# One gate block ahead of the first prompt tile, and twelve quarters beside it, in the later token groups of a hybrid decoder layer

## The reference, cut to what matters

```python
xn = _rms_norm(h, norm_mix)
qa, ka, va, qkv_b, z, a, b, gate_logits = split(xn @ w_in)
oa = sliding_window_attention(rope(qa), rope(ka), va, sinks)
cb = silu(short_conv(qkv_b))                    # 4 taps; q, k, v of the delta branch
ob = gated_delta(l2norm(q), l2norm(k), v, g, beta)   # chunks of 64 tokens, state S carried on
ob = gated_rms_norm(ob, z)
ga, gb = split(sigmoid(gate_logits), 2)         # 2 x 1024 columns
h = h + (ga * (oa @ w_oa) + gb * (ob @ w_ob)) @ w_out
h = h + (silu(rms(h) @ w_gate) * (rms(h) @ w_up)) @ w_down
```

## Time and profile before

| | |
|---|---|
| median of three runs | 3521.89 us |
| profiled execution, its own time | 3523.42 us |
| its span | 3521.6 us |
| TensorE busy with matmuls | 3421.5 us, 97% of the span |
| VectorE, ScalarE, GpSimd busy | 1729.7, 1256.8, 253.1 us |
| mean granted TensorE clock | 0.982 of full speed |

### The profile page before, as it was taken

How to read it: one execution, slowest core, us unless ns; L and a number is a source line. 1 busy time by engine, 2 the same in 40 slices (tenths; PEclk the granted TensorE clock), 3 DMA queues, 4 the chain that set the end, 5 groups by cost and what they waited for, 6 DMA issues and landing times. The chain is left out here.

```text
span 3521.6 us, 52950 instructions
## 1 busy us (share of the span) xinstructions
PE 3421.5 (97%) x21860; PEld 2906.4 (83%) x21860; DVE 1729.7 (49%) x3115; ACT 1256.8 (36%) x2414; POOL 253.1 (7%) x289
## 2 busy tenths in 40 slices
PE   6989999999999999999999999999999999999998
PEld 6877889999998777888878877888888877788886
DVE  3834435443446654554445744554345754454343
ACT  3322334321234544432234544432223544432222
POOL 1211100000003110000002101000000311000000
PEclk9888899999999999999999999999999999999999
DMA  4111102322233111333233211233234211233232
GB/s 172 59 34 50 31 27 88 99 84 89 86 126 111 62 43 49 114 95 97 90 138 115 74 37 49 91 107 96 96 103 153 79 42 43 78 114 96 96 96 81
DMA packets 88558, 298.66 MB, mean 85 GB/s; under 512 B 12272, under 2 KB 14272, under 8 KB 87664
## 3 DMA queue, kind: packets, MB, share of 16 engines
q1 hardware_dynamic: 88320, 295.28, 26.0%
HBM read 283.63 MB, written 12.62 MB: 84 GB/s over the span
## 5 line engine op out<-in xcount | busy, mean ns | idle before, releaser
L740 PE MATMUL bank<-hnT,wh 128*128 128x512 f32 (+1 forms) x3520 | 931.5, 352 | 0.0
L1685 DVE TENSOR_TENSOR wl<-raw,wh 128x1024 fp32r<-128x1024 f32 x480 | 594.8, 1240 | 656.5 <-ACT wh L1324 655.2
L740 PE MATMUL bank<-xnT,wh 128*128 128x512 f32 (+2 forms) x2560 | 743.3, 377 | 11.1 <-DVE d_dT L1938 5.1
L740 PEld LDWEIGHTS bank<-hnT,wh 128*128 128x128 f32 x3520 | 619.3, 188 | 91.4 <-issue 0.2
L1324 ACT CAST wh<-raw 128x1024 fp32r<-128x1024 f32 x480 | 500.4, 1043 | 390.8 <-PE bank L740 338.4
L740 PE MATMUL bank<-hnT,wl 128*128 128x512 f32 (+1 forms) x1760 | 622.2, 354 | 0.0
L740 PEld LDWEIGHTS bank<-xnT,wh 128*128 128x128 f32 x2560 | 450.6, 194 | 84.4 <-issue 13.3
L740 PE MATMUL bank<-hid,wh 128*128 128x512 f32 (+1 forms) x1760 | 468.3, 354 | 3.2 <-DVE wl L1685 2.1
L740 PE MATMUL bank<-xnT,wl 128*128 128x512 f32 (+2 forms) x1280 | 469.9, 367 | 0.0
L740 PEld LDWEIGHTS bank<-hnT,wl 128*128 128x128 f32 x1760 | 330.6, 188 | 45.8
L740 PEld LDWEIGHTS bank<-hid,wh 128*128 128x128 f32 x1760 | 309.6, 188 | 51.2 <-DVE wl L1685 4.0
(11 more groups left out here) (309 smaller groups left out, 3897.1 us busy)
## 6 DMA issues: line engine op xcount, KB each, us to landing
raw<-in_wstream SPq DMA_DIRECT2D x472, 512.0 KB, 3.5
xr<-in_x_prompt SPq DMA_DIRECT2D x16, 512.0 KB, 5.1
xT<-in_xT SPq DMA_DIRECT2D x4, 2048.0 KB, 11.6
hT<-in_xT SPq DMA_DIRECT2D x4, 2048.0 KB, 8.5
out_yp_out<-hT SPq DMA_DIRECT2D x16, 512.0 KB, 2.9
raw<-in_wstream SPq DMA_DIRECT2D x8, 528.0 KB, 3.6
Sb<-in_state_delta SPq DMA_DIRECT2D x1, 2048.0 KB, 10.3
out_ds_out<-Sb SPq DMA_DIRECT2D x1, 2048.0 KB, 6.8
```

The lines of the kernel that those rows point to most:

```text
L740: ins = nc.tensor.matmul(*a, **k)
L1685: v_.tensor_tensor(wl[n % HL][:, 0:m], raw[:, n % RAW, 0:m], wh[n % HL][:, 0:m].bitcast(F32), ALU.subtract).then_inc(sem("lo_done"), 1)
```

## The change

In groups 1 to 3 the first gate block is no longer spread over the first positions of tile 0. TensorE does it in one piece behind the last conv block, ahead of the transposes of tile 0, and ScalarE copies it (with the rounding of gate unit 2) ahead of everything of tile 0. Tile 0 keeps twelve quarters: positions 0, 1, 4 and 17 have one fewer each. Group 0 already had such a block ahead of its tile S and is not changed. The counts of tiles 1 to 3 are not changed either.

```diff
 QUARTERS = (1, 2, 1, 0, 2, 1, 1, 1, 0, 1, 1, 0, 1, 0, 1, 0, 1, 2)
 QUARTERS_C = 4
+QUARTERS_1 = (0, 1, 1, 0, 1, 1, 1, 1, 0, 1, 1, 0, 1, 0, 1, 0, 1, 1)
...
-        quarters_of = lambda t: QUARTERS_S if t == "S" else QUARTERS_0 if first else QUARTERS
+        quarters_of = lambda t: QUARTERS_S if t == "S" else QUARTERS_0 if first else QUARTERS if t else QUARTERS_1
...
# TensorE
+            for _ in range(QUARTERS_C):
+                gate_quarter()
             if first:
-                for _ in range(QUARTERS_C):
-                    gate_quarter()
                 pe.wait_ge(*made("conv_post", NCONV * (1 + F)))
                 delta_rows("S")
...
# ScalarE
-            quarters = [QUARTERS_C if first else 0]
-            if first:
-                gate_logits()
+            quarters = [QUARTERS_C]
+            gate_logits()
...
# VectorE
-            quarters = [QUARTERS_C if first else 0]
+            quarters = [QUARTERS_C]
```

More of the change, by code:

```diff
@@ L57 @@
 QUARTERS_S = (1, 1, 1, 1, 1, 1, 0, 0, 0, 0, 0, 0, 0, 2, 0, 0, 0, 0)
+QUARTERS_1 = (0, 1, 1, 0, 1, 1, 1, 1, 0, 1, 1, 0, 1, 0, 1, 0, 1, 1)
 QUARTERS_0 = (1, 1, 1, 0, 1, 1, 1, 1, 0, 1, 1, 0, 1, 0, 1, 0, 0, 2)
-assert sum(QUARTERS) * NT == 64 and QUARTERS_C + sum(QUARTERS_S) + sum(QUARTERS_0) * NT == 64
+assert QUARTERS_C + sum(QUARTERS_1) + sum(QUARTERS) * (NT - 1) == 64 and QUARTERS_C + sum(QUARTERS_S) + sum(QUARTERS_0) * NT == 64
 IN_DELTA = dict(inputs=2, scores=(3, 8), exp=(5, 10), transposes=(6, 11), values=(7, 13))
```

## The result

The changed kernel takes 3543.28 us (median of four runs, 3542.88 to 3546.42), against 3522.94 (3519.68 to 3525.91) for the kernel before beside it: a ratio of 1.0059, 95% interval 1.0046 to 1.0071. That is 20.3 us or 0.6% slower. The profiled execution has a span of 3541.3 us, 19.7 more than before. Its page shows the same work on TensorE; the busy row grows by 3 us.

The account below looks back on a forecast made before the run. TensorE's work plus its waits was taken to bound the kernel. 2.53 - 0.36 + 0.92 + 2.02 = 5.1 us per group, 15.3 for groups 1 to 3, plus 0.8 for the clock, gave 3538.0; range 3528 to 3545.

Parts of the forecast that it names:

- The front: Start of tile 0: L1052 starts 2.53 us later per group; bound 2.46 if `d_kTd` waits for its transposes alone.
- Positions 4, 5, 10 and 17: Tile 0, per group: position 4 gives back 0.36 us, completion at 5 costs 0.92, at 10 costs 2.02, position 17 gains 0.
- Rival A: Tile 0: only the start costs, exponentials at positions 5 and 10 aren't late; 6.5 us, so 3528.4; chance 0.07.
- Rival B: Tile 0: block fills the wait, exponentials and X ready as early as before; 8 us faster, 3514; chance 0.04.
- The clock: Waits of tile 0: TensorE's clock falls behind them; adds 0.8 us, half of one stretch; bounds 0 and 5 us.
- Rival C: Clock falls in each group, or late gate unit 4 makes ScalarE wait at position 10; 3539 to 3545; chance 0.09.
- The bank rule: By the rule alone, block behind conv block and positions 5 and 10 cost about 0.5 us each, 4 in all.

Follow-up runs that it names:

- The dose: Two, three or four quarters ahead of tile 0's transposes, completions at 6, 12 and 17, against the kernel before: 3523.45, 3527.38, 3534.72 us.
- Run 1: Changed kernel with one quarter of tile 0 moved from position 1 to 17, so blocks complete at 6, 12 and 17: 3534.72 us, ratio 1.0032.
- Run 3: Changed kernel with one quarter of tile 0 moved from position 10 to 17, so the third block completes at 12: 3538.88 us, ratio 1.0043.
- Run 4: Whole block at position 0 of tile 0, none ahead, VectorE's low part of gate unit 2 at position 1: 3524.26 us, 0.9997 of kernel before.
- two ahead: Two quarters ahead of tile 0's transposes, none at position 5, completions at 1, 6, 12 and 17: 3523.45 us, 0.9996 of kernel before.
- two at position 0: Two quarters at position 0 of tile 0, none ahead, none at position 5: 3523.42 us, 0.9997 of kernel before.

## Why the prediction was right, and its weakest term

The prediction said 3538.0 us with a range of 3528 to 3545, slower. Measured are 3543.28. Of the 5.3 us between them 1.0 is the kernel before, whose median was 3521.89 then and 3522.94 beside the change; 4.2 are the clock (5.0 for the 0.8 given) and 0.5 the chain, to within half a microsecond.

- **The front** was right to 0.02 us. The dose shows that the delay begins where the quarters ahead outlast ScalarE's last `post`. That the full block's delay runs through the wait of ScalarE's queue for its gate copy is seen on the rows (the copy starts at 2019.83, behind 1.00 of waiting). How much of it would stay if only the copy were moved was not tried; by the bound given, nearly all, since the transposes themselves come that late.
- **Positions 4, 5, 10 and 17** were right to 0.05 us each. Run 1 took the completions at 5 and 10 away, and both waits before L916 went. Run 3 took away that at 10 alone; the second wait fell from 1.98 to 0.81, and where the clock stayed up in both (group 3 of run 3, group 2 of the changed kernel) the second L916 is 38.91 behind `d_kn` against 40.96, 2.05 us less. Rival A (only the front costs) falls by run 1.
- **Rival B** (the block fills the wait and the tile does not notice) names what the change lacked. Run 4 meets its condition, the tile's chain as early as before, and is back at the kernel before. It doesn't gain the 8 us: L1053 waits 1.76 there, so the chain and not TensorE's work sets the front of tile 0.
- **The clock** was mis-sized. The step "I add 0.8 us, half of one such stretch" priced all new stretches together at less than one. Measured were four instead of one, 1.45 us each, 5.0 us more than the kernel before loses. The stated bound (one stretch per group, 5 us) was met in size, with another count behind it, two stretches in each of two groups; that the two agree is luck. With it the sum would have been 3542.2. The chain terms were short by a further 0.5 in all. The list of waits in that step was right. What was missed is that its two waits of 2 us are as likely places as the one of 2.17 us that had shown it, and that the stretch seen before had cost only 0.83 us because the wait of 0.65 behind it took up the rest, and little does so behind the new ones.
- **Rival C** (more than forecast) has the measured time in its band, 3539 to 3545, by its part on the clock, though the clock fell in two groups and not in each. Its other part, a weight unit that comes late at position 10, did not happen: in group 2 ScalarE rounds that unit at 2046.74, directly behind its copy of X, and then waits 2.07 us for TensorE's quarter. Groups 1 and 3 have the same wait of 2.07.
- That group 2 kept its clock in the changed kernel, and groups 1 and 3 in the kernel before, with the same waits, stays unexplained, and so does the fall in group 2 of run 3 behind waits of 0.65 and 0.81: the runs say where it can fall, not when it does.
- **The bank rule.** The Trainium skill, Perfetto Trace Analysis, section Optimizing Tensor Performance, advises rotating banks between matmul groups. The trace agrees that the same bank makes the next group wait (0.77 and 0.38 us), but the price depends on what stands behind the wait. The one of 0.38 was covered by the exponentials. The one of 0.77 was covered by slack with two quarters ahead; with four it stands in front of the block, the transposes and `d_kTd`, which follow each other without a gap, so by the rows it is a part of the 2.55 us. A block in another bank was not tried.

No version run here beats the kernel before beyond its interval. The nearest are two ahead (0.9996), two at position 0 and run 4 (0.9997 each).

## What to carry to other kernels

Work that is moved into a wait carries its shares on the other engines with it. Before counting the wait as filled, look at what each in-order queue holds behind the moved item's copy or conversion, and how far the item outlasts the wait: here two quarters (2.8 us) were free, the third cost 1.15 and the fourth 1.39 us per group. When work is dealt out in pieces, the position where a unit completes can matter more than where its pieces run: a completion just ahead of something that is waited for can cost the rest of the piece plus the copy (2.07 us at position 10 and 0.95 at position 5; nothing at position 17).

## What the runs showed of the hardware that was not expected

TensorE's clock fell to the 1.2 GHz level for about 3 us behind waits of only 2 us, and each such stretch cost 1.45 us, unless a wait stood behind it to take up a part (0.83 in the kernel before). It fell behind four of the six waits of 2 us in the trace of the changed kernel, and once behind waits of 0.65 and 0.81 (run 3, group 2). Seven matmuls that nobody reads, in each of the two waits, kept it at the 2.4 GHz level over the whole of tile 0 in all three groups (granted clock 1.00 from 1190 to 1260 us, 2000 to 2080 and 2810 to 2900) without moving the chain, and took 5.7 us off tile 0 and 4.4 us off the span.
